# Two-layer streaming encoder in float32 on one core: the loop of further expert blocks moved from behind the last turn to the front of the third, and three small reorderings

## The reference, cut to what matters

```python
D_MODEL, SEQ, DEPTH, MEM_LEN = 1024, 256, 2, 256       # 32 experts in 4 groups, 2 per token
for l in range(DEPTH):
    h = rms_norm(x, mix_norm[l])
    q, k, v, u, vg, cx, cb, cc, gl = split_columns(h @ w_in[l])
    ...
    gates = sigmoid(gl + b_gate[l])                     # three branches
    merged = (gates[:, :, 0] * (y_a @ w_branch[l, 0])
              + gates[:, :, 1] * (y_b @ w_branch[l, 1])
              + gates[:, :, 2] * (y_c @ w_branch[l, 2]))
    x = x + merged @ w_out[l]
    x = x + memory_cross_attention(rms_norm(x, xattn_norm[l]), rms_norm(mem, mem_norm[l]),
                                   w_xq[l], w_xkv[l], w_xo[l])
    x = x + hierarchical_moe(rms_norm(x, ffn_norm[l]), ...)   # (silu(x@w1a) * (x@w1b)) @ w2 per expert
return rms_norm(x, final_norm)
```

## Time and profile before

| | us |
|---|---|
| median of 3 runs | 1621.98 (1621.16 to 1622.59) |
| the profiled execution's own time | 1621.78 |
| its span | 1620.0 |
| PE busy (matmul) | 1307.8, 81% |
| DVE busy | 600.1, 37% |
| ACT busy | 450.4, 28% |

### The profile page before, as it was taken

How to read it: one execution, slowest core, us unless ns; L and a number is a source line. 1 busy time by engine, 2 the same in 40 slices (tenths; PEclk the granted TensorE clock), 3 DMA queues, 4 the chain that set the end, 5 groups by cost and what they waited for, 6 DMA issues and landing times.

```text
span 1620.0 us, 31268 instructions
## 1 busy us (share of the span) xinstructions
PE 1307.8 (81%) x13549; PEld 1014.9 (63%) x13549; DVE 600.1 (37%) x983; ACT 450.4 (28%) x661; POOL 0.4 (0%) x5
## 2 busy tenths in 40 slices
PE   6999999998668586787758999999987656667764
PEld 5999999996345262554428999998844323334432
DVE  6658755744131110212117885565431101111111
ACT  6445544633030110101015544454401001000101
POOL 0000000000000000000000000000000000000000
PEclk8999999999989897989978999999999889878987
DMA  9733456448999999999994635672799999999995
GB/s 355 258 136 127 156 207 228 190 157 361 415 426 426 423 427 422 427 421 426 427 380 145 250 131 182 221 260 105 279 413 428 426 427 426 428 427 421 426 427 224
DMA packets 91181, 520.00 MB, mean 321 GB/s; under 512 B 9754, under 2 KB 13218, under 8 KB 66212
## 3 DMA queue, kind: packets, MB, share of 16 engines
q1 hardware_dynamic: 90300, 515.94, 79.3%
q10 hardware_dynamic: 744, 2.05, 0.4%
HBM read 515.87 MB, written 2.10 MB: 320 GB/s over the span
## 4 chain that ended last, share of the span: by engine, by line
PE 52%; DMA 35%; DVE 6%; ACT 3%; issue 2%; SPq 1%; ACTq 0%; DVEq 0%
DMA ring<-in_w_expert_out 30%; PE banks L1689 27%; PE banks L2121 5%; PE banks L1719 5%; PE banks L2074 5%; DMA ring<-in_w_expert_in 4%; PE banks L2135 2%; DVE w_lo L1017 2%; SPq L509 1%; PE banks L2091 1%; ACT w_hi L640 1%; DVE stat L1470 1%; PE banks L1907 1%; PE banks L1844 1%; PE banks L1923 0%
## 5 line engine op out<-in xcount | busy, mean ns | idle before, releaser
L2074 PE MATMUL banks<-ring,arena 128*32 128x256 f32 x3904 | 272.5, 430 | 136.5 <-DMA ring<-in_w_expert_in 130.8
L2074 PEld LDWEIGHTS banks<-ring,arena 128*32 128x32 f32 x3904 | 127.4, 120 | 262.5 <-DMA ring<-in_w_expert_in 162.8
L1017 DVE TENSOR_TENSOR w_lo<-ring,w_hi 128x2048 fp32r<-128x2048 f32 (+1 forms) x105 | 215.1, 2049 | 126.3 <-ACTq L617 114.9
L1689 PE MATMUL banks<-h_hi,w_hi 128*128 128x256 f32 x776 | 221.8, 286 | 4.1 <-DVEq L1008 4.1
L1689 PE MATMUL banks<-h_hi,w_lo 128*128 128x256 f32 x776 | 219.5, 283 | 0.0
L2121 PE MATMUL banks<-ring,arena 128*32 128x256 f32 x2048 | 152.5, 448 | 80.8 <-DMA ring<-in_w_expert_out 69.4
L958 ACT ACTIVATE arena<-banks 128x128 f32<-128x128 f32 x66 | 18.4, 278 | 699.1 <-PE banks L2074 699.1
L1463 DVE TENSOR_TENSOR arena<-arena,banks 128x128 f32<-128x128 f32 x66 | 19.1, 289 | 511.6 <-ACT arena L958 511.6
L1689 PE MATMUL banks<-h_lo,w_hi 128*128 128x256 f32 x712 | 201.4, 283 | 0.0
L640 ACT CAST w_hi<-ring 128x2048 fp32r<-128x2048 f32 (+1 forms) x105 | 179.9, 1713 | 69.6 <-PE banks L1689 34.4
L2121 PEld LDWEIGHTS banks<-ring,arena 128*32 128x32 f32 x2048 | 76.6, 125 | 135.3 <-issue 71.4
(11 more groups left out here) (418 smaller groups left out, 2161.6 us busy)
## 6 DMA issues: line engine op xcount, KB each, us to landing
ring<-in_w_expert_in SPq DMA_DIRECT2D x122, 2048.0 KB, 23.5
ring<-in_w_expert_out SPq DMA_DIRECT2D x62, 2048.0 KB, 24.5
ring<-in_w_in SPq DMA_DIRECT2D x24, 2048.0 KB, 9.1
ring<-in_w_branch SPq DMA_DIRECT2D x12, 1024.0 KB, 5.2
ring<-in_w_out SPq DMA_DIRECT2D x4, 2048.0 KB, 8.3
ring<-in_w_xq SPq DMA_DIRECT2D x4, 2048.0 KB, 8.3
ring<-in_w_xo SPq DMA_DIRECT2D x4, 2048.0 KB, 8.6
arena<-in_w_xkv SPq DMA_DIRECT2D x4, 2048.0 KB, 25.6
```

The lines of the kernel that those rows point to most:

```text
L1017: post(dve.tensor_tensor(piece_view(w_lo, *key), piece_view(ring, *key), high_view(*key).bitcast(F32), ALU.subtract), "w_split")
L1689: ins = pe.matmul(acc, stationary(a, k), moving(b, k), start=k == 0 and n == 0, stop=k == kc - 1 and n == 2)
L2074: ins = pe.matmul(G[32 * j:32 * j + 32, :], tokens, w[:, k % 4, :, j * P:(j + 1) * P], start=k == 0, stop=k == KC - 1, tile_position=(0, 3 ...
```

## The change

Four edits are made together.

1. The loop of further blocks stands in front of turn 2 (the third) on all engines. SP reads the count when it comes to unit 48, after units 42, 43 and 44 are released; units 48, 49 and 50 then go to the slots of 45, 46 and 47, and the three kept slots are given back at once (with a count of 0), so that 51, 52 and 53 wait for nobody. At the end of a layer nothing is kept: q, kv and u go to the slots of units 90, 91 and 92. The second layer's loads are written out instead of looped.
2. At the start PE does the third K job (xk 2) ahead of the tokens' transposes; ACT casts the piece xv0,0 ahead of the tokens' evacuation; DVE splits xv0 and xv1,0 and does `k_part(2)`, `k_part(3)` before and around the scaling of the memory, and no split stands inside `norm`; ACT stores `mhat` behind `x_high`; SP waits for the scaled memory before it loads over it.
3. In the mix, ACT casts gate21's two pieces and br21,0 before it makes `merged_high(0)` and `(1)`, and casts wo0,0 before the sigmoid of gate21,1.
4. In the cross-attention, DVE does `o_part(0)` before `scale(2)`, and ACT's `exps(3)` comes behind the first evacuation of the attention's values.

```diff
+EXTRA_TURN = 2
+EXTRA_AT = 3 * EI * EXTRA_TURN
...
-    order = jobs(0, [..., ("memnorm", 1), ("x", 4), ("xk", 1, 2), ("norm0", 1), ("xk", 1, 3), ("xv", 4)])
+    order = jobs(0, [..., ("memnorm", 1), ("xk", 1, 2), ("x", 4), ("norm0", 1), ("xk", 1, 3), ("xv", 4)])
...
-            u = FIRST_EXPERT[layer] + n - (0 if first else SPARE[layer])
+            u = FIRST_EXPERT[layer] + n - (0 if first else SPARE[layer]) + (3 if n >= EXTRA_AT else 0)
...
+                def extra_loads():
+                    for x in range(3):
+                        slot_is_free(u1 + x)
+                    sp.sem_inc(X["used"], 1)
+                    sp.wait_ge(S["table_ready"], layer + 1)
+                    count = sp.value_load(tabi[0:1, 32:33], min_val=0, max_val=XB)
+                    with sp.If(count > 0):
...
+                    sp.wait_ge(X["used"], count + 1)
+                    for x in range(3):
+                        sp.sem_inc(slot_loaded[(u1 + x) % R], 16)
+
+                for n in range(head + R, 3 * NE):
+                    if n == EXTRA_AT:
+                        extra_loads()
+                    ring_unit(n)
...
# ACT, start
+            split_to(0, "xv0", 0, ahead=0)
             for i in range(4):
                 evac(0, "x", i, xT[:, 2 * i:2 * i + 2, :], "x_ready")
             n_x[0] += 1
-            split_to(0, "xv0", 0, ahead=0)
...
# ACT, gates
                             split_to(layer, f"gate{i}{h}", j)
+                            if (i, h, j) == (2, 1, 0):
+                                act.wait_ge(S["acc_ready"], JOB[layer, "br01", 1][1])
+                                merged_high(0)
+                                merged_high(1)
                             acc = job_wait(act, layer, f"gate{i}{h}", j)
+                            if (i, h, j) == (2, 1, 1):
+                                split_to(layer, "wo0", 0, ahead=0)
...
-                        if (i, h) == (1, 1):
-                            act.wait_ge(S["acc_ready"], JOB[layer, "br01", 1][1])
-                            merged_high(0)
-                            merged_high(1)
...
# DVE, start
+            split_to(0, "xv0", 0, ahead=0)
+            k_part(2)
+            split_to(0, "xv0", 1, ahead=0)
+            k_part(3)
             for i in range(4):
                 dve.wait_ge(S["mem_ready"], i + 1)
                 part = mem_T[:, 2 * i:2 * i + 2, :]
                 post(dve.tensor_tensor(part, part, mem_rstd.unsqueeze(1).broadcast_to([P, 2, T]), ALU.mult), "mhat_ready")
-            split_to(0, "xv0", 0, ahead=0)
-            k_part(2)
-            split_to(0, "xv0", 1, ahead=0)
-            k_part(3)
...
-                norm(ROW_MIX, layer, True, layer > 0, ("u" if layer else "xv1", 0))
+                if layer == 0:
+                    split_to(0, "xv1", 0, ahead=0)
+                norm(ROW_MIX, layer, True, layer > 0, ("u", 0) if layer else None)
...
# DVE, cross-attention
+                o_part(0)
                 scale(2)
-                o_part(0)
                 scale(3)
...
# PE, start
             token_norm("memnorm", mem_diag, 0)
+            dense(0, "xk1", "xk", m, i0=2, halves=(0,))
             turn_in("x", x_raw, "x_loaded")
-            dense(0, "xk1", "xk", m, i0=2, halves=(0,))
             token_norm("norm0", x_diag, TB)
...
# PE, experts (DVE and ACT alike)
+                def extra_turn():
+                    X = extra_sems[layer]
+                    pe.drain().then_inc(X["sel_used"], 1)
+                    pe.wait_ge(S["table_ready"], layer + 1)
+                    count = pe.value_load(tabi[0:1, 32:33], min_val=0, max_val=XB)
...
                 for turn in range(TURNS):
+                    if turn == EXTRA_TURN:
+                        extra_turn()
                     main_turn(turn)
```

More of the change, by code:

```diff
@@ L427, in slot_is_free @@
                 before = [key for key, n in UNIT_NO.items() if n == u - R]
-                reserved = any(0 <= u - R - FIRST_EXPERT[i] - 3 * NE + SPARE[i] < 3 for i in range(L))
+                reserved = any(0 <= u - R - extra_unit(i) < 3 for i in range(L))
                 if reserved:
@@ L553, in next_kv_load @@
                     sp.dma_start(kv_weight.rearrange("p (k n) -> p k n", k=KC), source(layer + 1, name)).then_inc(S["next_kv_loaded"], 16)
[L555 to L572, removed]
@@ L574, in _ @@
-                X = extra_sems[layer]
[L575 to L586, removed]
+                X = extra_sems[layer]
@@ new lines, in _ @@
+                u1 = extra_unit(layer)
+                def extra_loads():
[5 more added lines that the diff above has]
+                    with sp.If(count > 0):
+                        with sp.Fori(0, count) as k:
+                            e = expert_at(sp.value_load(tabi[0:1, bass.ds(k, 1)], min_val=0, max_val=NE - 1))
+                            sp.wait_ge(X["used"], k + 1)
+                            for x in range(3):
+                                expert_unit(ring[:, (u1 + x) % R, :], e, x, X["loaded"])
+                    sp.wait_ge(X["used"], count + 1)
+                    for x in range(3):
+                        sp.sem_inc(slot_loaded[(u1 + x) % R], 16)
@@ L587, in _ @@
+                for n in range(head + R, 3 * NE):
+                    if n == EXTRA_AT:
+                        extra_loads()
+                    ring_unit(n)
+                    if layer + 1 < L and n in KV_LOAD_BEHIND:
+                        next_kv_load(KV_LOAD_BEHIND.index(n))
                 for name in MIX_UNITS[:3] if layer + 1 < L else []:
                     load_dense(layer + 1, name)
-                sp.wait_ge(X["used"], count + 1)
-                for x in range(3) if layer + 1 < L else []:
-                    sp.sem_inc(slot_loaded[(u1 + x) % R], 16)
@@ L752, in _ @@
             split_to(0, "xv1", 0, ahead=0)
+            x_high()
+            split_to(0, "xv1", 1, ahead=0)
             act.wait_ge(S["mhat_ready"], 4)
             act.dma_start(mhat_dram, mem_T.rearrange("p a b -> p (a b)")).then_inc(S["mhat_stored"], 16)
-            x_high()
-            split_to(0, "xv1", 1, ahead=0)
             v_part(0)
```

73 lines of the change are left out of this document (40 added, 33 removed).

## The result

The changed kernel takes 1611.84 us (median of 4 runs, 1609.93 to 1613.02) against 1622.28 for the one before in the same series; the ratio is 0.9932 with a 95% interval of 0.9915 to 0.9949. A second series gave 1611.15 and 0.9928 (0.9915 to 0.9941). The prediction was 1609.8 with a range of 1605 to 1617. The profiled execution took 1613.02, with a span of 1610.6, 9.4 less than the 1620.0 of before.

The account below looks back on a forecast made before the run. It took the DMA queue to bound the expert parts and PE the dense parts; -1.9 - 5.4 - 1.6 - 2.3 + 3.1 + 0 - 4.1 = -12.2 from 1621.78 gave 1609.6, or 1609.8 against the median; range 1605 to 1617.

Parts of the forecast that it names:

- Start, -1.9: At the kernel's start, xk 2 fills PE's 5.75 us idle time, but DVE's later chain makes PE wait 3.6: -1.9 us.
- Mix, -5.4: In both layers' mix, earlier casts and splits end PE's waits before gate21 and wo0, 2.7 us a layer: -5.4 us.
- Cross-attention, -1.6: Before xo0's first product, PE's idle 1.45 us a layer ends, of which 0.8 a layer is kept: -1.6 us.
- End of layer 0, -2.3: PE's closing matmuls come 7.14 us earlier, but q's landing and three casts are late next: -2.3 us.
- One of the prediction's own signs of being wrong: At layer 0's end, the prediction is wrong if q starts more than 8.5 us behind the last weighted sum.
- End of layer 1, -4.1: Idle times of 1.29 and 2.51 us around the closing matmuls go, and DVE's last scaling starts earlier: -4.1 us.
- Hold, +3.1: Around unit 48, keeping three ring slots makes unit 49 land late in layer 0, +3.1 us; 0 in layer 1.
- rival (a): At the ring's hold, units 48 and 49 land as before, so it costs nothing: -15.3, 1606.7 us; chance 0.20.
- Branches, 0: In front of turn 2, PE's drain, load and branch take 7.1 us, hidden by units in flight: 0.
- Rival (d): PE's branch fetch queues behind weights in flight, lasts 24.5 us and starves the ring: +9, 1631 us; chance 0.05.

Follow-up runs that it names:

- The second profile: The changed kernel run again with the same code, in the same series as two further kernels, for another profile; ratio 0.9928 to the kernel before.
- turn 1: The changed kernel with the loop of further blocks in front of the turn numbered 1 and not 2; 1607.55 us, ratio 0.9914 to the kernel before.
- turn 3: The changed kernel with the loop of further blocks in front of the turn numbered 3 and not 2; 1628.86 us, ratio 1.0035 to the kernel before.

## Why the prediction was right, step by step

**Start, -1.9: right place, wrong size.** The wait of 3.6 with xv1's second half at 64.0 came as worked out (3.58, 64.00). The mis-sized term is the half clock behind it: I took one stretch of 3.4 for 1.3 us, and it was 6.83 for 2.6 us. Lead 0.6 and not 1.9. The second profile had the short stretch, so the term goes from one to the other between executions.

**Mix, -5.4: right.** The groups give back 3.1 and 1.8, the ledger 2.7 a layer. **Cross-attention, -1.6: right.** 2.4 of idle time went (2.9 to 0.5), 0.8 to 0.9 a layer arrived at the units asked for behind it; the rest is work in between.

**End of layer 0, -2.3: right** (2.0). The landing and the three casts are late next, as said: q starts 8.42 behind its unit's landing (844.78), forecast 8.43. One of the prediction's own signs of being wrong did come, though: q more than 8.5 behind the last weighted sum. It is 10.1 (843.11 to 853.20), since PE's last expert ran at the full clock here and ended 1.3 earlier than before (844.41), while the landing didn't move. The sign was tied to the wrong event; the path was the forecast one. **End of layer 1, -4.1: right**, 4.6 here; over the kernels with the loop moved, the span goes on for 13.4 to 15.3 us behind PE's last wait for weights (before: 18.0), so this edit is worth 2.7 to 4.6. The spread goes with the clock in the tail: its mean is 0.61 to 0.64 in the four kernels with 14.7 to 15.3, and 0.68 to 0.80 in those with 13.4. At the clock of the tail before (0.63) it is 2.7 to 3.3; the 4.6 of this profile is the upper end.

**Hold, +3.1: right, a little too dear.** 2.17 in layer 0; the 2.3 worked out from the 7.5 us of one unit was the better figure (n = 49 took 7.8 from issue to landing). So rival (a), a free hold, is out. The reason that I hadn't named is what ties up the release of units 45 and 46: the two K jobs for the next layer. It fits that layer 1, without them, lost only 0.4 in its whole expert part.

**Branches, 0: right for a wrong reason.** I took 7.1 us of stop, hidden behind the queue. The branch is 0.34 to 0.38, the stop 1.4 in layer 0. The long branch isn't a matter of a busy DMA: at the layer's end it was 6.08 to 6.21 us in three kernels at three times (the DMA engines at 0.97 in the kernel before), and at turn 1, 2 and 3, with the DMA engines at 0.89 to 1.02, it lasted between 0.34 and 1.57. In these runs it stays with one place in the instruction stream. The Trainium skill's rule (Runtime: NRT & Kernel Launch, Instruction fetch mechanics) fits this: the branch's target is in the fetched window or it isn't. The page speaks of the target's place and not of how busy the DMA is, which I had read into it. That the window decides was not tested alone. Layer 1's gather also stopped for 2.28 us, on no event that the profile shows, 4 to 6 us behind the branch; it does so for 2.1 to 3.7 us in all seven profiles with the loop in front of turn 2, and the cause isn't shown. Rival (d), in which this stop starves the ring, is refuted with it; but turn 3 shows that the ring can be starved by the kept slots alone, for more than the whole gain.

**What moved the sum from -12.2 to -9.4**, by the ledger: +1.3 for the start's clock, +1.5 for the stretch at 165, +0.4 where the queue of layer 0 fills, +0.2 at q's start, +0.4 for the clock behind it, +0.4 in layer 1's expert part; against them 0.9 on the hold and 0.5 on the tail. That is +2.8, all of the difference in this execution. Mix and cross-attention came out at their 7.0. The first two of these terms, 2.8 together, and the 0.5 go with the clock of the profiled execution. By the ratio of the medians the change is worth 11.0, and the 1.2 that this lacks of 12.2 isn't traced. So the mechanisms are shown term by term, but that the whole came within 2 us is in part luck: errors of 1.3 and 0.9 went opposite ways.

## What to carry to other kernels

A reservation in a ring of buffers costs what the queue can't cover while the ring is short, so it belongs where the consumer releases slots early: look at what else the consuming engine does in the two steps ahead of it. When a wait is taken from one engine, run the whole order of its feeder forward and see which item is now late; here a 3.2 us operation that nobody needed soon stood ahead of the one that PE wanted, and moving it was worth more than the reordering itself. And PE's stop of 3.6 us was worth its own length plus 1.3 to 2.7 us of half clock behind it, from one execution to the next.

## What the runs showed of the hardware

TensorE's clock fell to 1.2 GHz for 3.41 us near 165 with PE busy at 100% and no idle time ahead, in 7 of 13 profiles of kernels that are alike there (near 160 where all is 5 us earlier), and in one of two profiles of the very same code. The same happened near 950, in layer 1, in 2 of the 13. Each costs 1.5 to 1.6 us. Behind an idle time of 3.6 us the half clock lasted 3.41 or 6.83. A comparison of two single traces is uncertain by these 1.5 to 3 us, which is a third of the change measured here.
